# Recurrence of a streaming hybrid trunk: small products moved to the boundaries of the projections, state products ahead of stream states, and a second PSUM place for the first query projection

## What is computed

```python
proj = (h @ w_in).astype(jnp.float32)                 # h: tokens x 1024
q, fl, iv, g = jnp.split(proj, 4, axis=-1)
f = lb + (1.0 - lb) * jax.nn.sigmoid(fl)
k = 1.0 - f
# in blocks of HG_BLOCK tokens, per head:
    scores = jnp.einsum('bhtk,bhsk,bhtsk->bhts', qc, kc, decay)
    o = (jnp.einsum('bhts,bhsv->bhtv', scores, ic)
         + jnp.einsum('bhtk,bhkv->bhtv', qc * jnp.exp(bcum), s))
    s = (jnp.exp(b_last)[..., None] * s
         + jnp.einsum('bhsk,bhsv->bhkv', kc * jnp.exp(b_last[:, :, None] - bcum), ic))
o = o * lax.rsqrt(jnp.mean(o * o, axis=-1, keepdims=True) + EPS)
o = o.reshape(bsz, t, D_MODEL) * norm_w.astype(jnp.float32) * jax.nn.silu(g)
return o.astype(h.dtype) @ w_o, s_fin.astype(s0.dtype)
```

## Time and profile before

| what | value |
|---|---|
| median of 3 runs | 3151.37 us (3150.02 to 3156.91) |
| profiled execution, its own time | 3150.01 us |
| its span, first to last instruction | 3148.2 us |
| PE busy | 2945.1 us, 94% of the span |
| DVE busy | 1711.2 us, 54% |
| POOL busy | 839.2 us, 27% |
| ACT busy | 519.2 us, 16% |
| mean granted clock of PE | 0.973 |

### The profile page before, as it was taken

The page is one execution under the profiler, slowest core; times in us unless marked ns, Lnnn a source line. Parts: engine busy times, 40 slices in busy tenths (PEclk is TensorE's granted clock), DMA queues, the critical chain, the costliest instruction groups (busy, mean ns, idle before and its releaser), DMA issues.

```text
span 3148.2 us, 41516 instructions
## 1 busy us (share of the span) xinstructions
PE 2945.1 (94%) x16894; PEld 2850.9 (91%) x16894; DVE 1711.2 (54%) x1865; ACT 519.2 (16%) x643; POOL 839.2 (27%) x632
## 2 busy tenths in 40 slices
PE   6999979999999999978998989998899999999995
PEld 6888759999999999978998888998899999999994
DVE  7999951644444445564444444554264444445545
ACT  3011041211111111130111011112221111111112
POOL 5111114222232223251111111111522322232233
PEclk9999989999999999999999999999999999999997
DMA  3010121111111111121111001112111111111111
GB/s 125 24 30 22 25 77 37 41 40 46 40 40 46 41 40 40 47 97 35 42 35 42 28 27 42 35 35 100 35 41 40 40 47 40 40 40 47 40 40 65
DMA packets 63950, 141.28 MB, mean 45 GB/s; under 512 B 22256, under 2 KB 31984, under 8 KB 63856
## 3 DMA queue, kind: packets, MB, share of 16 engines
q1 hardware_dynamic: 36672, 107.49, 10.1%
q10 hardware_dynamic: 27184, 32.49, 3.0%
HBM read 123.89 MB, written 16.07 MB: 44 GB/s over the span
## 4 chain that ended last, share of the span: by engine, by line
PE 87%; DVE 7%; issue 3%; POOL 2%; ACT 1%; DMA 0%; ACTq 0%; DVEq 0%; POOLq 0%
PE BANKS L513 59%; PE BANKS L639 12%; PE BANKS L664 4%; PE BANKS L846 3%; PE BANKS L580 2%; DVE XL L1165 1%; POOL ARENA L448 1%; DVE HGA L1412 1%; PE BANKS L582 1%; PE BANKS L612 1%; DVE X L1237 1%; PE BANKS L730 1%; PE BANKS L707 1%; PE BANKS L605 1%; PE BANKS L689 0%
## 5 line engine op out<-in xcount | busy, mean ns | idle before, releaser
L513 PE MATMUL BANKS<-XH,WH 128*128 128x384 f32 x2688 | 617.8, 337 | 62.3 <-DVE XL L1165 42.2
L431 POOL TENSOR_TENSOR SMALL<-WRAW 128x1 f32<-128x1 f32 x196 | 53.0, 270 | 2235.0 <-PE BANKS L513 1542.4
L513 PE MATMUL BANKS<-XL,WH 128*128 128x384 f32 x2688 | 613.1, 335 | 0.0
L513 PE MATMUL BANKS<-XH,WL 128*128 128x384 f32 x2688 | 612.6, 335 | 0.0
L513 PEld LDWEIGHTS BANKS<-XH,WH 128*128 128x128 f32 x2688 | 479.8, 189 | 71.4 <-issue 46.9
L434 POOL TENSOR_TENSOR WL<-WRAW,WH 128x1024 fp32r<-128x1024 f32 x196 | 479.9, 2449 | 15.7
L513 PEld LDWEIGHTS BANKS<-XL,WH 128*128 128x128 f32 x2688 | 481.7, 189 | 0.0
L513 PEld LDWEIGHTS BANKS<-XH,WL 128*128 128x128 f32 x2688 | 481.5, 189 | 0.0
L1275 DVE TENSOR_TENSOR X<-BANKS,X 128x1152 f32<-128x1152 f32 x168 | 228.0, 1357 | 291.1 <-PE BANKS L513 211.2
L1328 DVE SCALAR_TENSOR_TENSOR ARENA<-ARENA 128x1168 f32<-128x1168 f32 x176 | 254.6, 1447 | 129.0 <-ACT ARENA L989 119.6
L989 ACT ACTIVATE ARENA<-ARENA 128x1168 f32<-128x1168 f32 x88 | 120.2, 1366 | 990.5 <-DVE ARENA L1187 990.5
(11 more groups left out here) (132 smaller groups left out, 3305.5 us busy)
## 6 DMA issues: line engine op xcount, KB each, us to landing
WRAW<-in_w SPq DMA_DIRECT2D x188, 512.0 KB, 3.2
X<-in_x SPq DMA_DIRECT2D x8, 576.0 KB, 8.8
X<-in_x ACTq DMA_DIRECT2D x8, 576.0 KB, 7.9
x_kept<-X ACTq DMA_DIRECT2D x8, 576.0 KB, 2.8
X<-x_kept ACTq DMA_DIRECT2D x8, 576.0 KB, 7.7
out_y<-X ACTq DMA_DIRECT2D x8, 576.0 KB, 3.2
HGA<-in_state ACTq DMA_DIRECT2D x8, 512.0 KB, 4.6
out_hgs<-HGA ACTq DMA_DIRECT2D x8, 512.0 KB, 2.6
```

The lines of the kernel that those rows point to most:

```text
L431: nc.gpsimd.tensor_tensor(PAD, one, one, ALU.mult)
L513: ins = nc.tensor.matmul(ps_bank(n, c), w, x[:, third(c)], start=(k == 0 and q == 0), stop=(k == last and q == 2))
```

## The change

The lines of the changed kernel are numbered anew: L639 becomes L648, L664 becomes L673, L730 becomes L739, L532 becomes L537, and on DVE L1412 becomes L1434, L1439 becomes L1461, L1461 and L1463 become L1483 and L1485, L1480 becomes L1511, L1483 becomes L1503.

It has these parts:

- On PE each boundary of two bigs has one small product in it: `scores(2)` between G and V, `scores(4 or 5)` between V and F, `scores(7)` between F and Q, and `outputs` between Q and the G of the next head. Before, the small products stood inside the bigs, and only `keys` and `outputs` stood at a boundary.
- `values` (VT) comes after three pieces of G (of V in head 6), not right after `outputs`.
- `state_steps` (DS) goes ahead of `stream_states` (NS).
- The first query projection, `("Q", 0)`, accumulates in banks 3 to 5 (`big_place`). Two of its pieces stand ahead of `stats`, and it no longer waits for DVE's copy of F.
- On DVE, `gated` is cut in two: the multiplication by the gate and the norm weights now comes ahead of `own`, before the row norms are known, and the multiplication by the row norms (`normed`) after `decayed(1)`. The copy of F moves ahead of `decayed(7)`. At the start the copies of F and Q move ahead of the clearing of `SC` and the mask.
- In the last head the parts are set anew, and the first pieces of the output projection are mixed with `outputs`, `sums`, `spread` and each other; two of the lows (`output_low`) come earlier.

```diff
@@ SMALLS
-    SMALLS += [("VT", _h)] + ([("SUM", _h - 1)] if _h else []) + [("L0", _h), ("L1", _h)]
-    SMALLS += ([("RB", _h - 1)] if _h else []) + [(f"L{_l}", _h) for _l in range(2, LEVELS)]
-    SMALLS += [(_n, _h) for _n in ("KT", "NS", "DS", "O")]
+    SMALLS += [("VT", _h), ("SUM", _h - 1), ("L0", _h)] if _h else [("L0", _h), ("VT", _h)]
+    SMALLS += [("L1", _h)] + ([("RB", _h - 1)] if _h else []) + [(f"L{_l}", _h) for _l in range(2, LEVELS)]
+    SMALLS += [(_n, _h) for _n in ("KT", "DS", "NS", "O")]
@@ new function
+        def big_place(what, h):
+
+            p = 1 if (what, h) == ("Q", 0) else 0
+            return PS[:, p * NCH:(p + 1) * NCH, 0:CW]
@@ part, on PE
-                    if a:
+                    if (what, h) == ("F", 0):
+                        emptied(pe, T_HG - 2)
+                    elif (what, h) == ("Q", 0):
+                        emptied(pe, T_HG - 1)
+                    elif (what, h) == ("V", 0):
+                        emptied_big(pe, "F", 0)
+                    else:
                         pe.wait_ge(a_free, a)
-                    else:
-                        emptied(pe, T_HG - 2)
@@ PE's order: the start
             part("F", 0, 0, KD, lows=P_HG)
+            part("Q", 0, 0, 2)
             stats(M_HG, Q_HG)
-            part("Q", 0, 0, KD)
+            part("Q", 0, 2, KD)
             part("V", 0, 0, KD)
+            scores(0, 0)
+            part("G", 0, 0, 3)
+            values(0)
+            part("G", 0, 3, 6)
+            scores(1, 0)
+            part("G", 0, 6, KD)
@@ PE's order: heads 1 to 5
             for h in range(HEADS - 2):
-                values(h)
-                part("G", h, 0, 2)
                 if h:
+                    part("G", h, 0, 3)
+                    values(h)
+                    part("G", h, 3, 4)
                     sums(h - 1)
-                scores(0, h)
-                part("G", h, 2, 5)
-                scores(1, h)
-                part("G", h, 5, 7)
-                if h:
+                    scores(0, h)
+                    part("G", h, 4, 6)
+                    scores(1, h)
+                    part("G", h, 6, 7)
                     spread(h - 1)
-                part("G", h, 7, KD)
-                part("V", h + 1, 0, 1)
+                    part("G", h, 7, KD)
                 scores(2, h)
-                part("V", h + 1, 1, 4)
+                part("V", h + 1, 0, 3)
                 scores(3, h)
-                part("V", h + 1, 4, 7)
+                part("V", h + 1, 3, 6)
                 scores(4, h)
-                part("V", h + 1, 7, KD)
-                part("F", h + 1, 0, 2)
+                part("V", h + 1, 6, KD)
                 scores(5, h)
-                part("F", h + 1, 2, 4)
+                part("F", h + 1, 0, 3)
                 scores(6, h)
-                part("F", h + 1, 4, 6)
+                part("F", h + 1, 3, KD)
                 scores(7, h)
-                part("F", h + 1, 6, KD)
+                part("Q", h + 1, 0, 2)
                 keys(h)
-                part("Q", h + 1, 0, 2)
+                part("Q", h + 1, 2, 4)
+                state_steps(h)
                 stream_states(h)
-                state_steps(h)
-                part("Q", h + 1, 2, KD)
+                part("Q", h + 1, 4, KD)
                 outputs(h)
@@ PE's order: heads 6 and 7 (h - 1 is 6 in the second list), the parts that the prediction names
+            part("V", h + 1, 7, KD)
             scores(2, h)
-            part("V", h + 1, 7, KD)
-            part("F", h + 1, 0, 1)
+            part("F", h + 1, 0, 2)
             scores(3, h)
...
+            part("G", h - 1, 7, KD)
             scores(2, h)
-            part("G", h, 1, 3)
+            part("G", h, 0, 2)
             scores(3, h)
...
+            scores(7, h)
             part("G", h, 7, KD)
-            scores(7, h)
             keys(h)
+            state_steps(h)
             stream_states(h)
-            state_steps(h)
-            outputs(h)
@@ PE's order: the output projection
             projected(0, 0, 2)
-            sums(HEADS - 1)
+            outputs(h)
             projected(0, 2, 4)
-            spread(HEADS - 1)
-            projected(0, 4, KD)
-            for m in range(1, KD):
+            sums(h)
+            projected(0, 4, 6)
+            spread(h)
+            projected(0, 6, 7)
+            projected(1, 0, 2)
+            projected(0, 7, KD)
+            projected(1, 2, KD)
+            for m in range(2, KD):
                 projected(m, 0, KD)
@@ DVE: gated in two
             def gated(h):
 
-                full_small(dve, "RB", h)
-                o = X[:, h, :]
-                V.tensor_tensor(o, small("RB"), o, ALU.mult).then_inc(s_free[small_place("RB")], 1)
-                emptied_small(dve, "RB", h)
+                emptied_small(dve, "O", h)
                 dve.wait_ge(gate_silu, h + 1)
-                V.scalar_tensor_tensor(out=o, in0=o, scalar=PAR[:, C_HGN, h:h + 1], in1=GATE,
-                                       op0=ALU.mult, op1=ALU.mult).then_inc(o_rdy, 1)
+                o = X[:, h, :]
+                return V.scalar_tensor_tensor(out=o, in0=o, scalar=PAR[:, C_HGN, h:h + 1], in1=GATE,
+                                              op0=ALU.mult, op1=ALU.mult)
+
+            def normed(h):
+
+                full_small(dve, "RB", h)
+                o = X[:, h, :]
+                mine()
+                V.tensor_tensor(o, small("RB"), o, ALU.mult).then_inc(s_free[small_place("RB")], 1)
@@ DVE's order: the start, and the places of the two halves and of F
+            projected("F", 0, FG)
+            projected("Q", 0, QFS[0])
             dve.wait_ge(mask_in, 16)
             dc.inc(V.memset(SC, 0.0))
             dc.inc(V.tensor_copy(MASK, VM))
             mine()
-            projected("F", 0, FG)
             forget(0)
             key(0)
-            projected("Q", 0, QFS[0])
+            totals()
             projected("V", 0, VF_FLAT)
...
-                totals()
+                if h:
+                    totals()
+                if 0 < h < HEADS - 1:
+                    dc.inc(gated(h - 1))
                 own(h)
                 if h:
                     diagonals(h - 1)
                 decayed(1, h)
+                if h:
+                    if h == HEADS - 1:
+                        emptied_small(dve, "O", h - 1)
+                    normed(h - 1)
...
-                for l in range(5, LEVELS):
-                    decayed(l, h)
+                decayed(5, h)
+                decayed(6, h)
                 if h + 1 < HEADS:
                     projected("F", h + 1, FG)
+                decayed(7, h)
+                if h + 1 < HEADS:
                     forget(h + 1)
                     key(h + 1)
                 else:
+                    dve.wait_ge(o_rdy, 1)
                     projected("G", h, GATE)
+                    for k in range(2):
+                        output_low(k)
```

More of the change, by code:

```diff
@@ L638, in part @@
                         for c in range(NCH):
-                            ins = nc.tensor.matmul(PS[:, c, 0:CW], w, x[:, k, third(c)],
+                            ins = nc.tensor.matmul(big_place(what, h)[:, c, :], w, x[:, k, third(c)],
                                                    start=(k == 0 and q == 0), stop=(k == KD - 1 and q == 2),
@@ L789, in _ @@
             scores(6, h)
[L790 removed]
+            part("F", h + 1, 6, KD)
             scores(7, h)
[L792 to L793 removed]
+            part("Q", h + 1, 0, 2)
             keys(h)
[L795 removed]
+            part("Q", h + 1, 2, 4)
+            state_steps(h)
             stream_states(h)
[L797 to L798 removed]
+            part("Q", h + 1, 4, KD)
             outputs(h)
             h = HEADS - 1
+            part("G", h - 1, 0, 3)
             values(h)
[L803 removed]
+            part("G", h - 1, 3, 4)
             sums(h - 1)
             scores(0, h)
[L806 removed]
+            part("G", h - 1, 4, 6)
             scores(1, h)
[L808 removed]
+            part("G", h - 1, 6, 7)
             spread(h - 1)
[L810 removed]
+            part("G", h - 1, 7, KD)
             scores(2, h)
[L812 removed]
+            part("G", h, 0, 2)
             scores(3, h)
[L814 removed]
+            part("G", h, 2, 4)
             scores(4, h)
+            part("G", h, 4, 5)
+            scores(5, h)
             part("G", h, 5, 6)
[L817 removed]
+            scores(6, h)
             part("G", h, 6, 7)
[L819 removed]
+            scores(7, h)
             part("G", h, 7, KD)
[L821 removed]
             keys(h)
+            state_steps(h)
             stream_states(h)
[L824 to L825 removed]
             def projected(m, k0, k1):
@@ L1092, in output_high @@
             def output_high(k):
-                act.wait_ge(o_rdy, k + 1)
+                if k == HEADS - 2:
+                    act.wait_ge(o_rdy, 1)
+                else:
+                    emptied_small(act, "RB", k)
```

(21 more changed lines are left out.)

41 lines of the change are left out of this document (13 added, 28 removed).

## The result

The changed kernel takes 3060.2 us (median of 4 runs, 3059.6 to 3062.1), the kernel before 3152.0 (median of 4). The ratio is 0.971, with a 95% interval of 0.970 to 0.972. The prediction said 3058 us, 3046 to 3090.

A forecast was written before the change was run, and what follows sets the result against it. PE, busy 94% of the span, bounds the kernel, so only its waits and low clock can go. Savings of 16.3, 54.0, 8.3 and 14.1 make 92.7 us off 3150.0: 3057.3, stated as 3058, range 3046 to 3090.

The forecast's parts named there:

- The boundaries: Between bigs: small products of 1.78 to 2.01 us cover the 1.55 until banks return; waits of 0.56, 2.63, 2.89 go.
- VT and the clock: Head starts: three pieces of G cover ACT's copy, 2.33 us goes; full clock from head 1 saves 3.7 each.
- The new wait at `spread`: Heads 1 to 7: PE waits 1.4 us at `spread` for the level-1 pick, 7 times.
- DVE beside POOL: Decays of levels 2, 5, 7 start inside POOL's subtraction: 1.35 us at `scores(3)` in heads 6 and 7, 0.15 at `keys`.
- DS ahead of NS: Costs nothing in heads 0 to 6; in head 7 PE waits 1.3 us at DS and some 0.3 at `outputs`.
- The start: Start with head 0: `stats` at about 1419.0, its lateness covered; 112.2 us against 128.5, 16.3 less.
- The sum: Start 16.3, heads 1 to 5 54.0, head 6 8.3, head 7 14.1: together 92.7 us less.
- the clock does not come back: Rival, chance 0.15: every head keeps its 3.7 us clock loss, 3088 us; half of it, 3073.
- the covers are too short: Rival, chance 0.12: each of some 23 boundaries costs up to a copy of 1.36 us, 31 us in all, 3089.
- the waits only change their place: Rival, chance 0.04: boundary products wait about as long themselves; only VT's 16.3 us and the start remain, about 3118.
- the exclusion of DVE and POOL grows until the kernel is slower: Rival, chance 0.04: delays at three new places per head grow into the next; slower needs 3.9 us at each.

The follow-up runs named there:

- first experiment: Changed kernel with the scores of levels 2, 5 and 7 one piece behind the boundary of two projections in heads 0 to 5: 3090.0 us.
- second experiment: Changed kernel with the transpose of the values right behind the outputs, not behind three pieces of the next projection, in heads 1 to 7: 3093.0 us.
- seventh experiment: Changed kernel with the spread of the row norms at the end of G (of V in head 6) and level 2 one piece later: 3051.7 us.
- sixth experiment: Changed kernel with POOL's split of the unit behind G, V and F held until DVE's decay multiplications of levels 2, 5 and 7: 3056.8 us.
- fifth experiment: Changed kernel with the stream states' product (NS) ahead of the state products (DS) again, in all heads: 3059.9 us.

## Why the prediction was right

**The boundaries.** Right. The first experiment brought back 18 waits of 1.54 us where I had worked out 1.55, and DVE was free when the bigs ended: in the changed kernel no big waits for its banks, and ahead of its copy of G DVE is idle for 0.23 us.

**VT and the clock.** The mechanism was right. The prediction took the clock loss per head as one sum of 3.7 us and did not say from which wait it came. The trace before gives 3.4, two stretches of 3.4 us at half clock (5.1 in head 3). The second experiment shows that a wait of 2.33 us at VT's place is enough by itself to bring half-clock stretches, 1.5 to 2.9 us of lost work at each wait. Waits of 1.4 to 1.5 us, even four in a head, bring none. Of the 12 us that a head lost before, the trace puts 2.3 of waiting and 1.7 of clock at VT; 6.1 of waiting and 1.7 of clock lie at the boundaries. No experiment brought waits of 2.9 and 2.6 us back by themselves. Nor does any say why the clock fell at every VT and only behind seven of the twelve waits of 2.6 to 2.9 us: that stays open.

**The new wait at `spread`.** Right: 7 x 1.36, forecast 1.4. It was an avoidable cost of this order, as the seventh experiment (the spread at the boundary of G) shows.

**DVE beside POOL.** The step was right in place and size: 21 of the 56 first decay multiplications, three in each of the heads 0 to 5, two in head 6 and one in head 7, started inside the subtraction and took 2.10 to 2.52 us, where the other 35 took at most 0.76. The waits at `scores(3)` in heads 6 and 7 were 1.2 us (1.35 forecast). In the kernel before, the same 56 took 42.6 us in all, so 33 us less than now; this is where the 28 us more of DVE's busy time come from, since other instructions there got shorter. At `keys` I had 0.15 us; the sixth experiment takes 0.3 from a head. That term was too small, 5 x 0.15 us over the heads. In all, the prediction put the exclusion at 3.8 us, and the sixth experiment gained 3.4.

The Trainium skill ("SBUF — State Buffer", Who interferes with whom) says that a DVE instruction with two SBUF inputs contends with a GpSimd instruction that reads SBUF, and that the contended port pair is an exclusive lock. The groups by form with and without the overlap agree: 76.0 and 41.8 us.

**DS ahead of NS.** The claim of nothing in heads 0 to 6 was right. In head 7 I took DS as what the states wait for in the expectation of the fifth experiment; it was DVE's two lows. The wait at the outputs came to 0.14 us where I had 0.3, the one ahead of DS to 1.22 where I had 1.3.

**The start.** `stats` at 1420.05, forecast 1419.0: the two pieces of Q ran at half clock as a whole, 5.9 us, where I had 4.8. From there to the end of head 0's outputs it took 100.9 us, forecast 101.3, so the sum was off by 0.6 us (112.8 against 112.2).

**The sum.** Forecast 92.7 us, measured 90.5 in the span. The misses: 0.6 at the start, 1.1 in heads 1 to 5, 0.7 in head 6, 1.2 in head 7, together 3.6. In heads 6 and 7 the waits in sum were no longer than forecast. What was too small there is the work of PE, busy for 69.1 and 161.4 us where the sum has 68.2 and 159.7. The part behind the recurrence was 1.4 us shorter (from 888.7 to 887.3), which no edit explains; the runs of the kernel before differ by 6.9 us among themselves. So the total came out closer than its terms by luck: 2.2 us off and not 3.6.

Of the rivals, that the clock does not come back and that the covers are too short are ruled out by the windows and the list of waits. That the waits only change their place holds for `spread` alone. That the exclusion of DVE and POOL grows until the kernel is slower is ruled out by the sixth experiment, where all of it is worth 3.4 us.

**What the parts are worth.** Undone one at a time: VT 33 us, boundary products of heads 0 to 5 30, cut of `gated` 9, second place with its two pieces 7, DS ahead of NS 0. That is 79 of 92 us. The worths need not add, since the clock's share depends on the other waits. Not undone by themselves are the new orders of heads 6 and 7 and of DVE's copies; that the rest lies there, or in what parts give only together, is argued and not shown.

## What to carry to other kernels

When an in-order engine must hand an accumulator over, put a short independent product at the hand-over that is a little longer than the copy, and then check from the consumer's order that it is idle at that moment: here DVE had 0.23 us to spare, and an instruction of 1.4 us more on it cost PE 1.4 us. Look in the trace at which waits the clock falls; here one wait of 2.3 us cost twice its own length, and four of 1.5 cost only themselves, but some of 2.9 us cost only themselves too. After such a change, look at what newly overlaps: a split on POOL beside multiplications on DVE, and one piece too few ahead of a product, together with a weight split that came late at the start, were the next 19 us.

## What the runs showed of the hardware

- The wait of 2.33 us at VT's place came with 3.4 or 6.8 us at half clock, seven times out of seven in the second experiment and again in the kernel before. Up to four waits of 1.4 to 1.5 us in each head never did (1.00 over 87.5 us, first experiment).
- Longer waits did not always: of twelve of 2.6 to 2.9 us in heads 0 to 6 of the kernel before, seven were followed by 3.4 us at half clock and five by none.
- Head after head was the same to the resolution of the window, 82.5 us, where before one of the five took 94.1 us and the others 92.7 to 92.9. The long one had three stretches at half clock, the others two.
- With POOL's subtraction moved away, 56 multiplications of DVE took 34 us less and a `TENSOR_SCALAR` (L1453) that now starts inside it took 14 us more, 2.57 us on average where it takes 0.76 alone; the kernel gained 3 us.
